# Stand-by products of 512 columns ahead of TensorE's waits in a two-block transformer kernel

## The reference, cut to what matters

```python
v = gc * u; y_conv = gb * conv3(v)                      # convolution of block 1
log_f = log_sigmoid(flog + fox_f_b)                     # its cumulated sum is a product with a triangle
...
o_na = neighborhood_attention(...)                      # block 2, each layer
o_gl = gla_bidirectional(q, k, v, la_f, la_b, s_f, s_b)
o_ga = gqa_latent_attention(...)
x = layer_norm(ALPHA * x + g1 * (o @ w_out), ln1_g, ln1_b)
x = layer_norm(ALPHA * x + g2 * swiglu(modulate(x, sh2, sc2), w_ffn_in, w_ffn_out), ln2_g, ln2_b)
```

## Time and profile before

| | us |
|---|---|
| median of 3 runs | 2501.4 |
| lowest and highest | 2499.85, 2502.88 |
| the profiled execution | 2500.61 |
| its span, first to last instruction | 2498.8 |

### The profile page before, as it was taken

How to read it: one execution, slowest core, us unless ns; L and a number is a source line. 1 busy time by engine, 2 the same in 40 slices (tenths; PEclk the granted TensorE clock), 3 DMA queues, 4 the chain that set the end, 5 groups by cost and what they waited for, 6 DMA issues and landing times. The chain is left out here.

```text
span 2498.8 us, 34079 instructions
## 1 busy us (share of the span) xinstructions
PE 2295.3 (92%) x13938; PEld 1496.6 (60%) x13938; DVE 959.1 (38%) x1773; ACT 637.2 (26%) x1028; POOL 135.8 (5%) x145
## 2 busy tenths in 40 slices
PE   6988899999999999999899877999999989888998
PEld 4866533344444344444487555678888777558997
DVE  2365321122111111211322756654344442756664
ACT  2333100011000010000332444342122252344433
POOL 0010000000000000000000232200000200211001
PEclk9989999999999999999999988999999999889999
DMA  9556899999999999999723522232332324434652
GB/s 301 169 169 202 328 406 428 428 428 428 428 429 429 428 429 428 428 429 428 283 91 131 170 90 93 83 101 70 110 101 75 101 93 140 136 118 126 181 174 93
DMA packets 264155, 606.13 MB, mean 243 GB/s; under 512 B 9808, under 2 KB 227920, under 8 KB 239344
## 3 DMA queue, kind: packets, MB, share of 16 engines
q1 hardware_dynamic: 264048, 604.61, 63.8%
HBM read 603.52 MB, written 1.05 MB: 242 GB/s over the span
## 5 line engine op out<-in xcount | busy, mean ns | idle before, releaser
L2002 PE MATMUL banks<-moe_ring,moe_x 128*64 128x512 f32 (+1 forms) x1920 | 351.2, 611 | 42.4 <-DMA moe_ring<-in_w_mlp 42.4
L2002 PEld LDWEIGHTS banks<-moe_ring,moe_x 128*64 128x64 f32 (+1 forms) x1920 | 116.7, 129 | 265.4 <-issue 264.7
L2211 DVE SCALAR_TENSOR_TENSOR res<-banks,mod,res 128x256 f32<-128x256 f32 x136 | 59.5, 479 | 519.1 <-PE banks L2023 501.2
L2562 PE MATMUL banks<-ff_xhi,ff_whi 128*128 128x512 f32 (+1 forms) x704 | 240.4, 342 | 13.6 <-DVE ff_xlo L2461 9.2
L2562 PE MATMUL banks<-ff_xhi,ff_wlo 128*128 128x512 f32 (+1 forms) x704 | 239.2, 340 | 0.0
L2562 PE MATMUL banks<-ff_xlo,ff_whi 128*128 128x512 f32 (+1 forms) x704 | 239.1, 340 | 0.0
L560 DVE TENSOR_TENSOR ff_wlo<-ring,ff_whi 128x2048 fp32r<-128x2048 f32 (+2 forms) x72 | 152.0, 2112 | 101.2 <-ACT ff_whi L551 98.9
L2104 ACT COPY moe_x<-banks 128x256 f32<-128x256 f32 x68 | 25.3, 373 | 591.3 <-PE banks L1962 591.3
L551 ACT CAST ff_whi<-ring 128x2048 fp32r<-128x2048 f32 (+2 forms) x72 | 126.4, 1756 | 124.9 <-PE banks L2594 118.4
L2562 PEld LDWEIGHTS banks<-ff_xhi,ff_whi 128*128 128x128 f32 x704 | 135.9, 193 | 31.3 <-DVE ff_wlo L560 13.9
L2562 PEld LDWEIGHTS banks<-ff_xlo,ff_whi 128*128 128x128 f32 x704 | 136.0, 193 | 13.9
(11 more groups left out here) (442 smaller groups left out, 3580.9 us busy)
## 6 DMA issues: line engine op xcount, KB each, us to landing
moe_ring<-in_w_mlp SPq DMA_DIRECT2D x128, 2048.0 KB, 17.0
ring<-in_w_mlp SPq DMA_DIRECT2D x64, 2048.0 KB, 15.7
ring<-in_w_ada SPq DMA_DIRECT2D x144, 512.0 KB, 4.6
ring<-in_w_ffn_in SPq DMA_DIRECT2D x88, 512.0 KB, 5.0
ring<-in_w_in SPq DMA_DIRECT2D x60, 512.0 KB, 4.6
ring<-in_w_out SPq DMA_DIRECT2D x24, 512.0 KB, 4.3
ring<-in_w_ffn_out SPq DMA_DIRECT2D x32, 384.0 KB, 3.1
ring<-in_w_ffn_out SPq DMA_DIRECT2D x16, 512.0 KB, 3.9
```

The source lines that it names most:

```text
L2002: mm = nc.tensor.matmul(u_bank[o][c:c + n_cols, :], x[:, 2 * kk + r, c:c + n_cols], self.moe_piece(2 * kk + m)[:, at:at + 512], start=Fals ...
L2211: return nc.vector.scalar_tensor_tensor(r, source, self.mod[:, 5, d, 0:1], r, ALU.mult, ALU.add)
L2562: mm = nc.tensor.matmul(bank[:, 0:width], w[:, k, :], xp[:, k, :], start=(k == 0 and term == 0), stop=(k == KC - 1 and term == 2))
```

## The change

Stand-by products are added at five kinds of places. In the convolution, 5 of 512 columns are issued ahead of the wait for L1537, into bank 0. The norm heads issue 8 instead of 4 of 512 columns, or 12 instead of 6 of 256. At the end of `window_and_gates`, 4 (layer 0) or 2 (layer 1) of 512 columns go into bank 0. Ahead of a stream's first coarse group, 6 (first stream of layer 0), 8 (its second) or 3 (layer 1) of 512 columns go into `ms_bank`; in the second stream a wait for the norm of the stream before comes ahead of them, because that norm is read from the same bank. Nothing is removed, and no DMA is touched.

```diff
@@ conv_and_gates, TensorE
                 for step in range(8):
                     self.side_step(pe, side, step)
+                self.keep_warm(self.bank[0], 5, 512)
 
                 pe.wait_ge(self.dve_ready.sem, self.dve_ready.at(3))
@@ head_tensor
             self.norm_tensor(pe, width, head["added"])
-            self.keep_warm(self.bank[5], 4 if width > S else 6, width)
+            self.keep_warm(self.bank[5], 8 if width > S else 12, width)
@@ window_and_gates
         width = S * v
+        context_out = l < LAYERS - 1
...
                                (self.sides_tensor(pe, side), n_side))
+                self.keep_warm(self.bank[0], 4 if context_out else 2, 512)
@@ queries_and_streams, TensorE
                 def coarse(y, s, c):
                     if c == 0:
+                        if y > 0:
+                            pe.wait_ge(self.dve_ready.sem, self.dve_ready.at(2 * y))
+                        self.keep_warm(ms_bank, (8 if y > 0 else 6) if len(streams) > 1 else 3, 512)
                         pe.wait_ge(self.hidden_ready.sem, self.hidden_ready.at(2 * y + 1))
```

## The result

| | us |
|---|---|
| median of 5 runs, changed kernel | 2489.3 (2484.9 to 2490.9) |
| before, beside it | 2501.4 (2499.9 to 2502.9) |
| ratio | 0.9948, 95% interval 0.9937 to 0.9959 |
| the profiled execution | 2490.91, span 2489.1 |

The kernel is 12.1 us faster; 17.1 were forecast for 2484, in a range of 2476 to 2496. A second timing beside other kernels gave 0.9949, 0.9934 to 0.9964.

The account below looks back on a forecast made before the run. TensorE, busy 92% of the span with its clock averaging 0.963, was taken as the bound. Gains of 2.7 + 2.4 + 4.2 + 2.8 + 4.0 + 1.0 = 17.1 us off 2501.4 gave 2484, range 2476 to 2496.

Parts of the forecast that it names:

- The price and the fit of the fills: All places: a 512-column product takes 0.86 us at full clock; no fill outlasts its wait, except the convolution's by at most 1.0.
- The rival that the fills are entered at half clock: All fills but the norm heads': 1.8 us a product outlasts each wait, 20.8 us later, 2522 with no gain; chance 0.04.
- Head transposes: Behind both joint-stage ends: transposes at full instead of half clock, 2.7 us gained in layer 0 and 2.4 in layer 1.
- the first rival: Behind three fills: the clock is lost again in the transposes, leaving a gain of 11.0 us, 2490; chance 0.15.
- The first stream: Layer 0: the first coarse group saves nothing, full clock behind it starts the first fine set 4.2 us earlier.
- the prediction's own signs: Streams: L3048 follows L3021 in about 10 us in the first; new ScalarE waits behind the coarse group would be wrong.
- Second stream and layer 1's: Coarse groups and the work behind at full clock: 2.8 us gained in layer 0's second stream, 4.0 in layer 1's.
- Norm heads: Three norm heads: time gained behind the fills is waited for later at VectorE's L2461, so 0; upper bound 7.8 us.
- The third rival: Norm heads pay too, because a bank or weight buffer frees sooner: up to 7.8 us more, 2476; chance 0.06.
- Convolution: The stage's end stays; the 24 transposes behind it gain 1.0 us, bounds a loss of 1.0 and a gain of 2.4.
- The reason named for the doubt: Convolution: TensorE finishes the short side products some 2 us before VectorE, so the clock can fall again before the transposes.

Follow-up runs that it names:

- e1_ends: Only the stand-by products at the two ends of window_and_gates, added to the kernel before; 2489.6 us, ratio 0.9961.
- e2_streams: Only the stand-by products ahead of the streams' first coarse groups, with their added wait, on the kernel before; 2491.9 us, ratio 0.9967.
- e6_between: The changed kernel plus a wait and two 512-column products ahead of the first stream's second coarse group, layer 0; 2481.9 us, ratio 0.9932 to the kernel before.
- e12_entry: e6_between plus three 512-column products in an early slot of layer 1's window stage; 2482.5 us, ratio 0.9928 to the kernel before.
- e3_heads: Only the longer fills of the three norm heads, added to the kernel before; 2500.6 us, ratio 1.0001.
- e4_conv: Only the five products in the convolution, added to the kernel before; 2501.1 us, ratio 1.0002.
- e7_double: The changed kernel with twice the stream fills (12, 16 and 6 products); 2490.3 us, ratio 0.9962 to the kernel before.
- e5_tiny: Kernel before plus fills at stage ends and streams only, 2-column products filling about the same time as the 512-column ones; 2500.3 us, ratio 1.0004.
- again: Second profiled execution of the unaltered changed kernel, from its timing beside other kernels; median 2487.1 us, ratio 0.9949 to the kernel before.
- e9_end1: Only the two products at the end of layer 1's window_and_gates, added to the kernel before; 2494.7 us, ratio 0.9981.

## Why the prediction was right, and where its terms were off

**The price and the fit of the fills.** Right. Four products are 3.68 us with their modelled tail, eight 7.13: 0.86 for each of the four more. None but the convolution's outlasted its wait, which put L1489 0.7 us late for the 1.0 allowed. The rival that the fills are entered at half clock fell: only the convolution's was, at 0.50 until 130.9 us; every other ran at 1.00 throughout.

**Head transposes.** Right: −2.2 for 2.7 and −2.8 for 2.4. With them the first rival fell: the clock stays at 1.00 through the 4.6 us that hold head transposes and nothing else of TensorE's. For transposes alone this stretch says less than the 24 rows of L897 in the earlier trace rows, behind which the clock is 0.98: of its 48 rows 16 are transposes (L929) and 32 are ordinary products with the identity (L932).

**The first stream: the term that failed, 4.2 forecast, 0.7 measured, and that not by its fill.** The prediction said that the first coarse group saves nothing because ScalarE takes up its copy only later, and in the next sentence let the clock be up for all that follows. The two belong together: a coarse group that ends sooner leaves TensorE waiting longer, 2.45 us for 1.26, and in that wait the clock fell and stayed at 0.50 for 10.2 us. The 0.7 is in e1_ends too, which has no fill here, and e2_streams, which has this fill, gave 0.0. e6_between filled the second wait and gave −4.5, at the forecast's own chain. The mechanism and the size were right; missing was a second uncovered wait. Two of the prediction's own signs show the miss: L3048 follows L3021 in 13.9 us, not in about 10, and the wait for ScalarE grew.

**Second stream and layer 1's.** Right in size: −2.3 for 2.8, −3.3 for 4.0. In layer 1 the clock fell once within the coarse group, to 0.50 for 3.4 us from 2192.5; where it did not (e2_streams) the stream gave 3.9. Neither is secured by its fill alone. The second stream gave only 0.5 and 0.6 in e2_streams and e12_entry, where the clock fell behind its first coarse group, and layer 1's gave 2.8 without a fill in e1_ends.

**Norm heads.** Right, 0, and e3_heads shows why. The third rival fell.

**Convolution.** 1.0 forecast, nothing that can be measured (e4_conv 1.0002). The reason named for the doubt is what happened: TensorE was done early and the clock had fallen, at 141.1 us, before the transposes, which in the changed kernel are at 0.54.

**What was not in the sum.** The clock also falls where nothing was changed, and where that fall lands moves with the program, and in e12_entry beside e6_between from one execution to the next. In layer 0's output projection it costs 1.5 us more than before; in layer 1's window stage 1.3 less, in the last pairs ahead of its output projection 1.6 less, in its last network 1.0 less. In layer 0's output projection such a fall lay over stand-by products before (first row); in the changed kernel it lies over the first real products (second row):

```profile
1563.90:1567.30 3.40, 3.40 (x5) 1.34 (x5) 1.72 (x1) 3.40 (x3) 0.00 (x0) 0.50 0.17 58
```
```profile
1567.90:1571.30 3.40, 3.26 (x8) 2.62 (x9) 3.40 (x4) 3.40 (x3) 0.00 (x0) 0.50 1.02 280
```

By the places of the table the changed kernel gains 13.7 and 13.9 us from the first pair on in its two profiled executions (−9.7 and −14.6 in all, +4.0 and −0.7 of it ahead of them), and the medians say 12.1 and 12.7. The forecast's 17.1 less the 3.5 of the first stream and the 1.0 of the convolution is 12.6, but that this meets the time is partly luck: the places with a term gave 11.3 of the 16.1 us forecast for them, and the places without one, where nothing was changed, gave 2.4 more on balance.

Ahead of the first pair the two executions of the changed kernel are 4.7 us apart, half of it in the first 50 us and half in the experts, so single profiled executions can't be compared by their totals, only place by place.

**Two slips above.** In the prediction the chances under 2496.4 us, 0.58, 0.15, 0.06 and half of 0.17, add up to 0.875, not 0.86. And the change has four kinds of places, not five.

## What to carry to other kernels

The stand-by products of these runs paid where two things held: they stood in a wait long enough to hide them (with twice the products the second stream ended 6.3 us late in e7_double), and the work behind the wait was bound by TensorE (behind layer 0's stage end it was busy 4.56 of 4.6 us before). Where another engine was waited for again a few microseconds later (the norm heads, 1.0001), the faster clock turned into a longer wait, 2.19 us in the first head. Look for both, and for the next uncovered wait as well, since the work in between ends sooner than before: the largest step beyond the change (e6_between, 0.9932) came from filling the one that the change itself had lengthened. And read such a change by the shift of like products from place to place, since the total of one execution mixes it with where the clock's other falls happen to land.

## What the runs showed of the hardware that was not expected

- Behind products of 2 columns that occupied TensorE's record for 3.66 us the clock was 0.50 (e5_tiny, ahead of layer 0's head transposes); behind products of 512 columns for 3.68 us it was 1.00 (the changed kernel).
- With a short group of small products (1.8 us at full clock) between a fill and a wait of 2.45 us, the clock fell to 0.50 for 10.2 us in three executions of three (changed, again, e2_streams); with two products of 512 columns in that wait it was 1.00 for the next 10 us.
- Times also changed at places where nothing was changed: with the two products at layer 1's stage end (e9_end1) stretches up to 120 us later changed by 1.0 to 1.6 us each. And the clock's falls are not the same in every execution: the second stream gave 2.3 us in e6_between and 0.6 in e12_entry, with the same code up to there.
